# The v gathers and their sums 24 slots behind the u gathers instead of 16

## The reference

```python
def chunk(xc):                                   # 128 tokens
    q = (xc @ w_q).reshape(128, 8, 256)
    s1 = einsum('chd,nd->chn', q[..., :128], keys1)
    s2 = einsum('chd,nd->chn', q[..., 128:], keys2)
    # top 16 of each, top 16 of their pair sums: idx (128, 8, 16), g = softmax
    u = u_tab[idx]
    a = gelu(einsum('chkd,cd->chk', u, xc))
    return einsum('chk,chkd->cd', g * a, v_tab[idx])
```

## Time and profile before

| | us |
|---|---|
| median of 3 runs | 2775.36 |
| lowest and highest run | 2770.03, 2795.08 |
| profiled execution: span from first to last instruction | 2774.0 |

### The profile page before, as it was taken

The page is one execution under the profiler, slowest core; times in us unless marked ns, Lnnn a source line. Parts: engine busy times, 40 slices in busy tenths (PEclk is TensorE's granted clock), DMA queues, the critical chain, the costliest instruction groups (busy, mean ns, idle before and its releaser), DMA issues.

```text
span 2774.0 us, 21455 instructions
## 1 busy us (share of the span) xinstructions
PE 1439.9 (52%) x6942; PEld 642.3 (23%) x6942; DVE 1533.6 (55%) x3968; ACT 335.9 (12%) x660; POOL 1478.9 (53%) x1546
## 2 busy tenths in 40 slices
PE   7886753546656654455334443369763333333333
PEld 3455310123313431122001110036541000000000
DVE  1328677667654555555665554326376666466442
ACT  1421110112201110110001000015110000000000
POOL 0004666665665465655666666600156666666664
PEclk9997876767778886667666765689876665665556
DMA  9628999998999899999999999940399999999997
GB/s 351 219 76 310 384 406 359 365 347 300 354 404 352 323 381 405 404 405 391 403 354 373 405 389 376 352 157 22 114 344 365 365 363 368 370 351 369 368 371 272
DMA packets 282574, 928.49 MB, mean 335 GB/s; under 512 B 27601, under 2 KB 28385, under 8 KB 282209
## 3 DMA queue, kind: packets, MB, share of 16 engines
q0 software_dynamic: 221184, 805.40, 76.0%
q1 hardware_dynamic: 61280, 121.73, 12.0%
HBM read 925.98 MB, written 1.05 MB: 334 GB/s over the span
## 4 chain that ended last, share of the span: by engine, by line
POOL 23%; PE 20%; DMA 19%; DVE 17%; issue 14%; another core or an unknown queue 6%; ACT 2%; SPq 1%; POOLq 0%; DVEq 0%; ACTq 0%
POOL RING L609 23%; DMA RING<-in_p_u,IDX 10%; DMA RING<-in_p_v,IDV 9%; DVE RING L692 7%; PE acc L1164 5%; PE wk L1226 4%; PE wk L1364 3%; PE wk L1349 3%; PE wk L1150 1%; DVE TI L681 1%; DVE TV L678 1%; PE wk L1308 1%; PE acc L1266 1%; DVE OHR L945 1%
## 5 line engine op out<-in xcount | busy, mean ns | idle before, releaser
L692 DVE SCALAR_TENSOR_TENSOR RING<-RING,acc 128x1024 f32<-128x1024 f32 x768 | 916.7, 1219 | 644.8 <-DMA RING<-in_p_u,IDX 527.3
L1164 PE MATMUL acc<-RING,ST 128*32 128x512 f32 x3072 | 617.5, 935 | 1057.7 <-DMA RING<-in_p_v,IDV 933.0
L609 POOL DMA_INDIRECT RING<-in_p_u,IDX x768 | 737.0, 960 | 690.8 <-DVE WG L956 404.2
L609 POOL DMA_INDIRECT RING<-in_p_v,IDV x768 | 740.3, 964 | 586.1 <-issue 208.0
L1164 PEld LDWEIGHTS acc<-RING,ST 128*32 128x32 f32 x3072 | 121.1, 147 | 1456.6 <-issue 1441.2
L1364 PE MATMUL wk<-HT,WR 128*128 128x256 f32 x768 | 188.9, 408 | 35.1 <-issue 20.4
L1364 PEld LDWEIGHTS wk<-HT,WR 128*128 128x128 f32 x768 | 157.1, 207 | 71.3 <-issue 45.4
L1226 PE MATMUL wk<-WR,HT 128*128 128x512 f32 x256 | 117.5, 616 | 5.9 <-DMA WR<-in_o_w_in 3.7
L1396 PE MATMUL wk<-SELW,WE 128*128 128x512 f32 x96 | 76.1, 886 | 82.0 <-DVE WE L713 71.2
L1123 ACT ACTIVATE GA<-A 128x16 f32<-128x16 f32 x48 | 10.3, 216 | 826.5 <-issue 416.7
L678 DVE MAX8 TV<-SCR 128x8 f32<-128x128 f32 x192 | 41.9, 281 | 83.5 <-ACT SCR L1114 55.2
(11 more groups left out here) (177 smaller groups left out, 1494.0 us busy)
## 6 DMA issues: line engine op xcount, KB each, us to landing
WR<-in_ada_w SPq DMA_DIRECT2D x31, 1024.0 KB
WR<-in_p_w_q SPq DMA_DIRECT2D x24, 1024.0 KB
RING<-in_ada_w SPq DMA_DIRECT2D x17, 1024.0 KB, 12.9
WR<-in_o_w_in SPq DMA_DIRECT2D x14, 1024.0 KB
RING<-in_p_u,IDX POOLq DMA_INDIRECT x768
RING<-in_p_v,IDV POOLq DMA_INDIRECT x768
WR<-in_e_w_in SPq DMA_DIRECT2D x8, 1024.0 KB
WR<-in_e_w_out SPq DMA_DIRECT2D x7, 1024.0 KB
```

The lines of the kernel that those rows point to most:

```text
L609: pool.indirect_dma_start(out=ring[:, n % NU, :], out_offset=None, in_=tables[table], in_offset=bass.IndirectOffsetOnAxis(ap=rows, axis=0) ...
L692: nc.vector.scalar_tensor_tensor(out=U[:, s % NU, :], in0=U[:, s % NU, :], scalar=1.0, in1=acc[:, 1, :], op0=ALU.mult, op1=ALU.mult, accum ...
L1164: ins = nc.tensor.matmul(acc[32 * g:32 * g + 32, 0, hf * 512:hf * 512 + 512], ST[:, c % 2, s, :], V[:, s % NV, hf * 512:hf * 512 + 512], s ...
```

## The change

The lag of v behind u is a constant, VLAG, in steps of four slots: 6 of them, 24 slots. v_quarter gives, for step n of a stage, the chunk and quarter of v that is gathered and summed in it (none in the first 6 steps); v_rest lists the six quarters that are left after the last step. GpSimd and TensorE use these. turned is now awaited where v's quarter 0 is reached. The update of a finished tile moves from step (0, 3) to step (1, 2) of the next tile, again behind the dots. In fills0 the norm of layer 1's context moves by one step (73 to 74), and layer 1's first latent norm, turn, projections, rotation and gate by three (100 to 115 become 103 to 118). The number and size of all instructions and gathers are the same.

```diff
+VLAG = 6
...
-    put(f, 73, ("normA", 1, 1, 2), ("normA", 1, 1, 3))
+    put(f, 74, ("normA", 1, 1, 2), ("normA", 1, 1, 3))
...
-    put(f, 100, ("normA", 1, 1, 0))
-    put(f, 101, ("normB", 1, 1, 0))
-    put(f, 102, ("hT", 1, 1, (0,)))
-    for n, c in zip((103, 105, 107), (2, 0, 1)):
+    put(f, 103, ("normA", 1, 1, 0))
+    put(f, 104, ("normB", 1, 1, 0))
+    put(f, 105, ("hT", 1, 1, (0,)))
+    for n, c in zip((106, 108, 110), (2, 0, 1)):
         put(f, n, ("in", 1, c, (0,)))
-    put(f, 110, ("rope", 1, 0, "qk", 1))
-    put(f, 111, ("rope", 1, 0, "qk", 2))
-    put(f, 113, ("tqk", 1, 0, "q"), ("tqk", 1, 0, "k"))
-    put(f, 115, ("bc", 1, LAT, G1))
+    put(f, 113, ("rope", 1, 0, "qk", 1))
+    put(f, 114, ("rope", 1, 0, "qk", 2))
+    put(f, 116, ("tqk", 1, 0, "q"), ("tqk", 1, 0, "k"))
+    put(f, 118, ("bc", 1, LAT, G1))
...
+def v_quarter(l, n):
+
+    return divmod(n - VLAG, 4) if n - VLAG >= 128 * l else None
+
+
+def v_rest(l):
+
+    end = 4 * (chunk0(l, ORDER[l][-1]) + PH)
+    return [divmod(n, 4) for n in range(end - VLAG, end)]
...
                     if q == 0:
                         pool.wait_ge(chosen.sem, chosen.at("topk", l, tile, h // 2))
-                        if c > 32 * l:
-                            turned(l, c - 1)
-                    for s_ in range(4 * q, 4 * q + 4):
-                        gather_u(c, s_)
-                        if c > 32 * l:
-                            gather_v(c - 1, s_)
+                    late = v_quarter(l, 4 * c + q)
+                    if late and late[1] == 0:
+                        turned(l, late[0])
+                    for s_ in range(4):
+                        gather_u(c, 4 * q + s_)
+                        if late:
+                            gather_v(late[0], 4 * late[1] + s_)
                 elif s[0] == "experts_end":
                     l = s[1]
-                    c = chunk0(l, ORDER[l][-1]) + PH - 1
-                    turned(l, c)
-                    for s_ in range(TOPK):
-                        gather_v(c, s_)
+                    for c, q in v_rest(l):
+                        if q == 0:
+                            turned(l, c)
+                        for s_ in range(4 * q, 4 * q + 4):
+                            gather_v(c, s_)
...
-                    if tile != ORDER[l][0] and (h, q) == (0, 3):
+                    if tile != ORDER[l][0] and (h, q) == divmod(VLAG, 4):
                         update(l, ORDER[l][ORDER[l].index(tile) - 1])
...
-                    c = chunk0(l, tile) + h
-                    if c > 32 * l:
-                        vsums(c - 1, q)
+                    late = v_quarter(l, 4 * (chunk0(l, tile) + h) + q)
+                    if late:
+                        vsums(*late)
                 elif kind == "experts_end":
-                    c = chunk0(s[1], ORDER[s[1]][-1]) + PH - 1
-                    for q in range(4):
+                    for c, q in v_rest(s[1]):
                         vsums(c, q)
```

## The result

The changed kernel takes 2786.72 us (median of 20 runs, 2779.9 to 2800.1), the kernel before beside it 2775.43 (20 runs). The ratio is 1.0036, 95% interval 1.0021 to 1.0051: about 10 us slower, where 5.1 faster was forecast. The range of 2747 to 2802 holds it, the sign is wrong, and the time is that of rival A (2786.3). The profiled execution after has a span of 2778.1 us, 4.1 above the one before.

A forecast was written before the change was run, and what follows sets the result against it. The gather stages were taken as bound by the chain gather, landing, dot or sum, free slot, next gather. Ends +7.9, copies -8, update -8, turn +2, norm +1 gave -5.1: 2770.3 us for the run, range 2747 to 2802.

The forecast's parts named there:

- rival A: Steady stretch: the transfers are the bound anyway and the middle gains nothing; 2786.3 us, chance 0.17.
- Tails: End of each stage: eight more v gathers run alone, 13.6 and 14.3 us, together +27.9 us.
- estimate of 19.2: Both tails priced at bytes over 436 GB/s with the fixed 2 us overlapped: 9.6 us per eight gathers, +19.2.
- Starts: Start of each stage: u24 to u29 issue earlier and long v-ring waits go; 9 and 11 us come back, -20.
- Late copies, -8: Steady stretch: sums no longer wait for ScalarE's late weight copies; -8 us, between 0 and -15.0.
- about half is given back: Steady stretch: of 15.0 us of pauses behind late copies, about half returns as "remote" pauses, leaving -8.
- Update, -8: Finished tile's update, moved to (1, 2): VectorE no longer waits there for sums; -8 us, between 0 and -20.5.
- Turn and norm: Next tile's first sums wait for the update, +2 us (0 to +10); layer 1's first norm delays dots, +1 (0 to +3).
- the sign that I named for "wrong": Behind the update at (1, 2): v-ring pauses of more than 2 us would show the forecast wrong.
- 82.0 us before L1396: TensorE's wait before the transposed weights: about as now if the forecast is right.
- Rival D: TensorE still waits for the newest chunk's weights, holding sums; copy term 2, update 4: +4.9, 2780.3 us, chance 0.13.
- Rival B: Starts give nothing back as VectorE binds the first six steps, tails cost in full, middle gains nothing: 2806.3 us, chance 0.10.

The follow-up runs named there:

- first pair: Traces of the changed kernel and the kernel before from the result's own job; profiled span 2778.1 us, 4.1 above the one before.
- repeated pair: The second pair of traces: both kernels run again unedited in a later job; ratios to the kernel before 1.0016 (changed kernel) and 0.9978 (kernel before).
- g: Both kernels with every second v quarter behind a stage's last u gather put into the u ring's slots; 0.9972 (changed kernel) and 0.9941 (kernel before).
- g1: The changed kernel with sixteen slots in the tails, every second v quarter there using the u ring; ratio 0.9972 to the kernel before.
- e1: The changed kernel with lag 24 from each stage's start, brought back to 16 near its end by two steps with eight v gathers each; ratio 1.0030.
- e4: The changed kernel with the tile update at step (1,1), in which the last sums run, instead of one step behind them; ratio 1.0052.
- h1: The changed kernel with v gathers of 512 and not 1024 values a row, every instruction kept; ratio 0.9547 to the kernel before.
- g pair: Traces of lag 24 against lag 16, both with sixteen-slot tails; ratios to the kernel before 0.9972 and 0.9941.
- e3: The changed kernel with lag 16 at both ends of each stage and 24 between, update and norm as changed; ratio 1.0009 to the kernel before.
- e: Four variants of the changed kernel trying ends, middle and update apart; ratios to the kernel before 1.0030, 1.0039, 1.0009 and 1.0052.
- h: Both kernels with v gathers of 512 and not 1024 values a row; ratios to the kernel before 0.9547 (changed kernel) and 0.9502 (kernel before).
- g2: The kernel before (lag 16) with sixteen slots in the tails, every second v quarter there using the u ring; ratio 0.9941.
- j3: g2 run once more in a job with remote waits; ratio 0.9961 to the kernel before.

## Why the prediction was wrong

The time was forecast 5.1 us lower and came out 10 higher, and the sum of the pieces says where. In the first pair the tails are +26.0 (27.9 forecast), the starts -13.4 (-20), the middles -7.6 (-13), and -0.9 lies between the layers: +4.1 for -5.1. Two steps failed. The first took the starts' gain as it stood at u29 for a gain that is kept. The second took about half of the pauses counted in the middle as gained (-8 for the copies, -8 for the update). The repeated pair has -15.9 for the starts and only -2.5 for the middles.

**Tails.** Right. 27.9 forecast, 13.2 + 12.8 = 26.0 measured in the first pair and 26.5 in the second. The last u gather comes 51 and 52 us before the last sum's end (50 to 54 forecast). The estimate of 19.2 by the Trainium skill's price ("DMA: Bandwidth & Descriptors", section Anatomy of one DMA) is missed by the eight-slot tails; the tails of 16 slots in g come to 20.4.

**Starts.** Too large: 20 forecast, 13.4, 15.9, 17.6 and 16.6 measured. The step that failed is not the reading at u29, where the kernel after is 9.4 and 11.3 us ahead ("the two long v-ring waits that lie before those rows go" is true of those rows). It is "I take 9 and 11" for the stage: the working ends at u29, and the first v gather that needs a sum, v8, comes behind u32. There GpSimd waits 8.27 and 8.43 us, since the sums of step 6 stand behind the same score work, and at the 65th u gather 5.0 and 8.4 us are left.

How long this wait is goes with ScalarE's late copies, which the prediction did not bring in here. In the jobs without them (and without "remote" waits) the kernels with a lag of 24 at the start do not have it; that the copies are the cause is argued from the order on TensorE and was not isolated. The ninth v gather of each layer in g1:

```profile
292.23 1.34 POOL L645 DMA_INDIRECT RING<-in_p_v,IDV  x1 [0.30 <-issue]
...
1977.72 0.94 POOL L645 DMA_INDIRECT RING<-in_p_v,IDV  x1 [0.30 <-issue]
```

In e1, e4 and h1 both are 0.30 as well. There layer 1 keeps its start (-13.6 in the g pair); layer 0 loses 5.8 of 9.8 us, behind pauses of 3.20 and 4.93 us at v12 and v16. And even there a start does not pay over the whole run: the eight v gathers that are not issued in it have to be issued elsewhere, at 1.24 us or more each, and e1 against e3 gives the lag of 24 at the starts a cost of 5.4 us.

**Late copies, -8.** The mechanism held (chunk 44 above), the size did not. The middle of layer 1, where most of the four copies are, gained 3.6 and 3.7 us in the two pairs with remote waits, and about 0 (+0.7, -0.8) in those without: in the eight traces of e, g and h not one copy begins over 5 us behind the start of its product, in each of the others 8 to 17 of 48 are. The failing step is "about half is given back". At chunk 44 all of it is: three "remote" waits, 5.1 us, in place of 5.89. Of the 15.0 us at least three quarters came back, and in a job without late copies there is nothing to gain. The 3.6 us hold the fourth update too, and 2.7 of them lie between u640 and u672, around it, so how much is the copies' is not shown. Nor are the late chunks the same from trace to trace: in layer 1 33, 36, 41 and 44 are over 10 us late before, 39 and 44 after.

**Update, -8.** The failing step is that the waits of VectorE count. They are gone, but GpSimd was held only behind the first of the four, and e4, which brings such waits back, shows no cost that can be told from nothing. The reading had a fault as well: of the 7.22 and 9.39 us of idle time put down to sums, 3.7 and 5.6 lie behind the end of the last of these sums in the rows. Where the first update lies, from u144 to u160, lag 24 gains 5.3, 4.6, 3.5 and 0.3 us in the four pairs, and keeps it only in part. In the first it is 7.2 us ahead at u144, 12.4 at u160, 10.6 at u240 and 9.0 at the last u gather; in the second 15.9, 20.5, 12.0 and 9.8; in the third 3.6, 7.1, 3.3 and 4.6. The long v-ring pauses of the middle stand at the same steps at either lag, for they are behind layer 0's long blocks on TensorE: in chunks 13 and 14, by the score blocks of steps 51 to 58, 15.0 and 10.6 us before, 13.8 and 10.8 after. In the second pair 6.9 us are lost from u176 to u240, where these two lie, in the first nothing; that they take in what came early is not shown. The first of them, after:

```profile
864.40 0.94 POOL L621 DMA_INDIRECT RING<-in_p_v,IDV  x1 [13.78 <-PE acc L1178]
```

**Turn and norm.** +2 and +1 were not separated. A pause of 9.12 us ends 6 us behind the second update, the sign that I named for "wrong", and TensorE's sums in front of it had waited for that update. The next pause is 3.6, and before the two at these steps were 5.3 and 5.9, so some 1.5 us went there.

**The other signs.** The 82.0 us before L1396 are 95.4, a little more, not as now. "Remote" waits fell from 171.3 to 120.3 us, but not in the second pair (150.1 and 154.3): for the kernel before alone the two traces differ by 21 us, so that the change does anything to them is not shown. Rival D is out, since sums no longer wait for the newest copy. Rival B is out: u24 was on time, and the starts are ahead. Rival A gave the right time, 2786.3, with the tails and starts of the forecast and nothing for the middle. That is luck in part: the starts gave less than it has, and in this pair the middle gave something. Its reason, that the transfers bind, is right in part too: h shows that without that bound the middle gains little either (2.9 us), because GpSimd's issues, at 1.24 us a gather, are as near. And the tenth between 406 and 365 GB/s, which the prediction has as holes against rival A, is hardly touched by the lag (369); in the jobs without "remote" waits it is not there at either lag (407 in g2, 406 in g1).

The medians say +10 and the first pair's traces +4.1, because the execution profiled after is the fastest of its twenty. The second pair's traces have +6.8. How the 10 us split between starts and middle is therefore open by several us; that the tails cost 26 and the rest gives back less than that is shown by both pairs.

## What to carry to other kernels

When two streams share one issuing engine, running one further behind the other never removes an item: it moves items from the start, where they run beside the other stream, to a tail, where each costs its full pace, and it pays only if the middle has waits of its own that nothing else will fill. Read the middle's pace per item against the slowest stage of the chain (in e3 1.31 us against 1.24) before counting pauses. Do not end the working of a start at the last row that looks good: go on to the first item that waits under the new order (here v8, three u gathers on). If a tail runs on half of the buffers because its partner stream has ended, give it the partner's buffers: the tail of sixteen slots at the old lag (g2, 0.9941 and, as j3, 0.9961) beats the kernel before in both jobs that it ran in.

## What was not expected of the hardware

The same kernel takes 2614 us in one job and 2786 in another on the same chip, with the granted clock alike (0.71 to 0.73). The difference goes with what the traces of the two kinds of job show: GpSimd's "remote" waits (none against 120 to 181 us) and late ScalarE copies (none against some of 12 to 16 us). Windows of layer 1's middle move 404 to 407 GB/s at a share of 1.02 in the one kind and 362 to 369 at 0.95 to 0.97 in the other. What sets it was not found; whether other cores of the chip were at work is not on record.
